# Group C's guests spread over more beats of the projection, and decode's page numbers read ahead of their wait

## What is computed

```python
h = rms_norm(x, norm_g)
proj = jnp.einsum('btd,dn->btn', h, w_in)
(aq, ak, av, az, bq, bkv, bg, bz, cqk, cv, cif, co, cz) = jnp.split(proj, splits, axis=-1)
...
oa = diff_attention(...)                                  # group A, paged cache in decode
o_cs, o_win = compressed + selected, banded window        # group B
...
for j in range(CONV_W):                                   # group C: causal convolution, 4 taps
    acc = acc + xp[:, j:j + T].astype(f32) * c_conv_w[j].astype(f32)
qk_c = jax.nn.silu(acc)
...
hc, (C1, n1, m1) = mlstm_chunkwise(qc, kc, vc, gif[:, :, 0], gif[:, :, 1], C0, n0, m0)
...
y = x + jnp.einsum('btm,md->btd', mix, w_out)
```

## Time and profile before

| | before |
|---|---|
| median of 3 runs (lowest to highest) | 2131.74 us (2131.07 to 2131.77) |
| profiled execution, its own time | 2134.85 us |
| its span | 2133.1 us |
| PE busy | 1754.7 us (82%) |
| PE weight loads busy | 1350.9 us (63%) |
| DVE busy | 819.9 us (38%) |
| ACT busy | 590.2 us (28%) |
| POOL busy | 81.1 us (4%) |
| HBM over the span | 170 GB/s |

### The profile page before, as it was taken

The page is one execution under the profiler, slowest core; times in us unless marked ns, Lnnn a source line. Parts: engine busy times, 40 slices in busy tenths (PEclk is TensorE's granted clock), DMA queues, the critical chain, the costliest instruction groups (busy, mean ns, idle before and its releaser), DMA issues. The chain is left out here.

```text
span 2133.1 us, 39056 instructions
## 1 busy us (share of the span) xinstructions
PE 1754.7 (82%) x14961; PEld 1350.9 (63%) x14961; DVE 819.9 (38%) x1592; ACT 590.2 (28%) x1352; POOL 81.1 (4%) x130
## 2 busy tenths in 40 slices
PE   7999999999886889879927975877787777647999
PEld 5888887888664556666716664555665655426776
DVE  4222212222264421234255752444455544646221
ACT  4211111112122102111134320444444444343110
POOL 3000000000000000000022010000000000021000
PEclk9999999999998877789967975999999999869999
DMA  6555655543322111132361002999899999455233
GB/s 198 175 185 182 189 159 184 179 135 105 125 83 66 59 44 60 55 87 82 100 254 54 29 21 82 361 341 337 311 331 329 355 321 331 166 195 192 80 122 110
DMA packets 213184, 361.28 MB, mean 169 GB/s; under 512 B 41229, under 2 KB 121566, under 8 KB 211142
## 3 DMA queue, kind: packets, MB, share of 16 engines
q1 hardware_dynamic: 212214, 356.16, 49.4%
q10 hardware_dynamic: 288, 2.10, 0.3%
q0 software_dynamic: 496, 0.53, 0.1%
HBM read 326.18 MB, written 36.79 MB: 170 GB/s over the span
## 5 line engine op out<-in xcount | busy, mean ns | idle before, releaser
L364 PE MATMUL pj_ps<-pj_whi,pj_xhi 128*128 128x512 f32 (+1 forms) x1024 | 420.9, 411 | 9.6 <-PEq L84 7.3
L365 PE MATMUL pj_ps<-pj_wlo,pj_xhi 128*128 128x512 f32 (+1 forms) x1024 | 404.7, 395 | 0.0
L366 PE MATMUL pj_ps<-pj_whi,pj_xlo 128*128 128x512 f32 (+1 forms) x1024 | 404.0, 395 | 0.0
L282 DVE TENSOR_TENSOR pj_wlo<-pj_w,pj_whi 128x1024 fp32r<-128x1024 f32 (+1 forms) x128 | 153.1, 1197 | 542.7 <-ACT pj_whi L242 540.3
L242 ACT ACTIVATE pj_whi<-pj_w 128x1024 fp32r<-128x1024 f32 (+1 forms) x128 | 132.6, 1036 | 578.7 <-DMA pj_w<-in_w_in 578.6
L364 PEld LDWEIGHTS pj_ps<-pj_whi,pj_xhi 128*128 128x128 f32 x1024 | 200.1, 195 | 70.3 <-issue 32.0
L366 PEld LDWEIGHTS pj_ps<-pj_whi,pj_xlo 128*128 128x128 f32 x1024 | 199.6, 195 | 41.2
L365 PEld LDWEIGHTS pj_ps<-pj_wlo,pj_xhi 128*128 128x128 f32 x1024 | 200.8, 196 | 34.5
L1347 PE MATMUL da_tp<-all_ident,da_pa 128*128 128x128 f32 x1024 | 156.1, 301 | 78.2 <-DMA da_pb<-in_cache_b_kv 76.7
L1467 ACT ACTIVATE da_kT<-da_tp 128x512 f32<-128x512 f32 x200 | 119.2, 596 | 263.0 <-PE da_tp L1347 263.0
L1347 PEld LDWEIGHTS da_tp<-all_ident,da_pa 128*128 128x128 f32 x1024 | 125.5, 154 | 99.5 <-DMA da_pb<-in_cache_b_kv 87.4
(11 more groups left out here) (513 smaller groups left out, 2231.8 us busy)
## 6 DMA issues: line engine op xcount, KB each, us to landing
da_pa<-in_cache_a_kv SPq DMA_DIRECT2D x256, 512.0 KB, 5.7
pj_w<-in_w_in SPq DMA_DIRECT2D x120, 512.0 KB, 4.6
px_pages<-in_cache_b_kv SPq DMA_DIRECT2D x256, 128.0 KB, 2.4
da_pb<-in_cache_b_kv SPq DMA_DIRECT2D x256, 128.0 KB, 6.1
ou_w<-in_w_out SPq DMA_DIRECT2D x32, 512.0 KB, 4.1
proj<-pj_out SPq DMA_DIRECT2D x52, 256.0 KB, 3.5
ap_rows_p<-proj SPq DMA_DIRECT2D x4, 1408.0 KB, 14.6
da_pw<-in_state_b_win SPq DMA_DIRECT2D x8, 512.0 KB, 7.8
```

The costliest lines, as they stand in the source:

```text
L282: dve.tensor_tensor(self.wlo[:, r, :, 0:n], self.w[:, r, :, 0:n], self.whi[:, r, :, 0:n], ALU.subtract).then_inc(self.wlo_ready, 1)
L364: pe.matmul(acc, hi, high, start=kc == 0, stop=False)
L365: pe.matmul(acc, hi, low, start=False, stop=False)
L366: last = pe.matmul(acc, lo, high, start=False, stop=kc == KC - 1)
```

## The change

It has five parts. (1) Decode: SP reads a group's four page numbers before it waits for `summed`, not behind. (2) `Convolve` has slots 80 to 99: its first four jobs come after 3 beats, the other ten after 20; the taps are 32 steps of one channel with a `yield` behind three of four, 24 beats in all; PE, ACT and DVE count their beats to match. (3) `PromptMemory` has slots 100 to 115: units follow each other every 5 beats (UNITBEATS) in place of 3, HEADBEATS goes from 9 to 11, PE and ACT start two beats later, PE gets a beat more behind the scores and behind the sums, and DVE makes denominator and output first, and the state (L2269, L2273 after) and mp_ncabd (L2207 after) one beat later. (4) `SampleMemory` has slots 116 to 127 and starts after 8 beats in place of 4. (5) The ranges of slots. No operation is added or taken away; `tapped` is raised 32 times in place of 8.

```diff
--- before.py
+++ after.py
@@ -1258,13 +1258,13 @@
                 for n, (b, what, p) in enumerate(steps):
                     if what == "page":
                         m = b * NG + p
+                        _, pages = nc.values_load_multi_w_load_instructions(
+                            table[0:1, 4 * m:4 * m + 4], engines=[mybir.EngineType.SP],
+                            min_val=0, max_val=d.cache_b.shape[0] - 1)
                         if m >= RING:
                             old = next(x for x in range(N) if steps[x][1] == "page"
                                        and steps[x][0] * NG + steps[x][2] == m - RING)
                             sp.wait_ge(summed, old + 1)
-                        _, pages = nc.values_load_multi_w_load_instructions(
-                            table[0:1, 4 * m:4 * m + 4], engines=[mybir.EngineType.SP],
-                            min_val=0, max_val=d.cache_b.shape[0] - 1)
                         for i in range(4):
                             sp.dma_start(pa[:, m % RING, i, :], d.cache_a[bass.ds(pages[i], 1), :, :]
                                          .rearrange("a p n -> p (a n)")).then_inc(loaded[m % RING], 16)
...
@@ -1817,16 +1816,20 @@
             yield
         sp.wait_ge(self.stored, 16 * (DB + 1))
 
-    START = 14
+    EARLY, START, TAPS = 3, 20, 24
+
+    def pause(self, n):
+
+        return self.EARLY if n == 0 else self.START - self.EARLY - 4 if n == 4 else 0
 
     def pool(self, pool):
         return iter(())
 
     def pe(self, pe):
         k = self.k
-        for _ in range(self.START):
-            yield
         for n, (what, t, h) in enumerate(self.JOBS):
+            for _ in range(self.pause(n)):
+                yield
             if what == "w":
                 pe.wait_ge(self.w_loaded, 48)
                 src, rows = self.w, 5
@@ -1856,7 +1859,7 @@
                                 k.ident[0:NS, 0:NS])
         last.then_inc(self.g_turned, 1)
         yield
-        for _ in range(8 + 4):
+        for _ in range(self.TAPS + 4 + 2):
             yield
         for t, (r0, rows) in enumerate(TILES):
             if t == 0:
@@ -1871,16 +1874,16 @@
 
     def act(self, act):
         k = self.k
-        for _ in range(self.START + self.N + 3):
+        for _ in range(self.START + self.N - 4 + 3):
             yield
         act.wait_ge(self.f_ready, 1)
         act.activation(self.t1[:], self.t0[:], ACT.Exp).then_inc(self.f_exped, 1)
         act.wait_ge(self.f_exped, 1)
         act.activation(self.t1[:], self.t1[:], ACT.Ln, bias=1.0).then_inc(self.f_logged, 1)
-        for _ in range(8):
+        for _ in range(self.TAPS):
             yield
         for x in range(4):
-            act.wait_ge(self.tapped, 8)
+            act.wait_ge(self.tapped, 32)
             if x:
                 act.wait_ge(self.silu_done, x)
             act.activation(self.sig[:], k.qkT[:, 2 * x:2 * x + 2, :], ACT.Sigmoid).then_inc(self.sig_done, 1)
@@ -1919,20 +1922,20 @@
         dve.scalar_tensor_tensor(self.t0[:], k.gate_f[:], -1.0, k.gate_f[:], ALU.mult, ALU.min).then_inc(self.f_ready, 1)
         yield
         dve.wait_ge(self.copied, self.N)
-        for x in range(8):
-            j, c0 = x // 2, 4 * (x % 2)
+        for x in range(32):
+            j, c = x // 8, x % 8
             if j:
-                dve.wait_ge(self.tapped, x - 1)
-            for c in range(c0, c0 + 4):
-                outs = ((k.qkT[:, c, 0:SEQ], self.xp[:, c, j:j + SEQ]),
-                        (k.qkT[:, c, SEQ:ROWS].rearrange("p (b t) -> p b t", b=DB), self.xs[:, c, :, j:j + DT]))
-                for out, src in outs:
-                    if j == 0:
-                        last = dve.tensor_scalar(out, src, self.wT[:, c, 0:1], self.wT[:, c, 4:5], ALU.mult, ALU.add)
-                    else:
-                        last = dve.scalar_tensor_tensor(out, src, self.wT[:, c, j:j + 1], out, ALU.mult, ALU.add)
+                dve.wait_ge(self.tapped, x - 7)
+            outs = ((k.qkT[:, c, 0:SEQ], self.xp[:, c, j:j + SEQ]),
+                    (k.qkT[:, c, SEQ:ROWS].rearrange("p (b t) -> p b t", b=DB), self.xs[:, c, :, j:j + DT]))
+            for out, src in outs:
+                if j == 0:
+                    last = dve.tensor_scalar(out, src, self.wT[:, c, 0:1], self.wT[:, c, 4:5], ALU.mult, ALU.add)
+                else:
+                    last = dve.scalar_tensor_tensor(out, src, self.wT[:, c, j:j + 1], out, ALU.mult, ALU.add)
             last.then_inc(self.tapped, 1)
-            yield
+            if x % 4:
+                yield
         dve.wait_ge(self.f_logged, 1)
         step(dve.tensor_scalar(k.gate_f[:], k.gate_f[:], 0.0, None, ALU.min))
         step(dve.tensor_tensor(k.gate_f[:], k.gate_f[:], self.t1[:], ALU.subtract))
@@ -2163,9 +2172,8 @@
                 h = 4 * hf + x
                 last = act.activation(self.w[:, x, :], self.bx[:, P * x:P * x + P], ACT.Exp, bias=self.col[:, c, 0, h:h + 1])
             last.then_inc(self.exped, 1)
-            yield
-            yield
-            yield
+            for _ in range(self.UNITBEATS):
+                yield
 
     def dve(self, dve):
         k, V = self.k, self.V
...
@@ -2237,20 +2247,12 @@
             dve.tensor_tensor(self.w[:], self.by[:].rearrange("p (x n) -> p x n", x=4), self.w[:],
                               ALU.mult).then_inc(self.weighed, 1)
             yield
+            yield
             dve.wait_ge(self.summed, u + 1)
-            for y in range(2):
-                half = slice(DC * y, DC * y + DC)
-                sy = self.S[half, 2 * hf:2 * hf + 2, :]
-                last = dve.tensor_tensor(sy, sy, self.csb[half, c, 4 * hf + y:4 * hf + 4:2].unsqueeze(2).broadcast_to(
-                    [DC, 2, V]), ALU.mult)
             nums = [b[:, 0:2 * V].rearrange("p (x n) -> p x n", x=2) for b in (self.bx, self.by)]
             for y in range(2):
-                dve.tensor_copy(self.den[:, 0, y:4:2].unsqueeze(2), nums[y][:, :, HEAD:V])
+                last = dve.tensor_copy(self.den[:, 0, y:4:2].unsqueeze(2), nums[y][:, :, HEAD:V])
             step(last)
-            st = self.S[:, 2 * hf:2 * hf + 2, :]
-            dve.tensor_tensor(st, st, self.bz[:, 0:2 * V].rearrange("p (x n) -> p x n", x=2),
-                              ALU.add).then_inc(self.state_ready, 1)
-            dve.wait_ge(self.state_ready, u + 1)
             step(dve.scalar_tensor_tensor(self.den[:, 1, :], self.den[:, 0, :], -1.0, self.den[:, 0, :], ALU.mult, ALU.max))
             step(dve.tensor_tensor(self.den[:, 1, :], self.den[:, 1, :], self.col[:, c, 1, 4 * hf:4 * hf + 4], ALU.max))
             step(dve.reciprocal(self.den[:, 2, :], self.den[:, 1, :]))
@@ -2260,6 +2262,16 @@
                 last = dve.tensor_tensor(self.h_out[:, y:4:2, :], nums[y][:, :, 0:HEAD],
                                          self.den[:, 2, y:4:2].unsqueeze(2).broadcast_to([P, 2, HEAD]), ALU.mult)
             last.then_inc(self.h_ready, 1)
+            yield
+            for y in range(2):
+                half = slice(DC * y, DC * y + DC)
+                sy = self.S[half, 2 * hf:2 * hf + 2, :]
+                last = dve.tensor_tensor(sy, sy, self.csb[half, c, 4 * hf + y:4 * hf + 4:2].unsqueeze(2).broadcast_to(
+                    [DC, 2, V]), ALU.mult)
+            step(last)
+            st = self.S[:, 2 * hf:2 * hf + 2, :]
+            dve.tensor_tensor(st, st, self.bz[:, 0:2 * V].rearrange("p (x n) -> p x n", x=2),
+                              ALU.add).then_inc(self.state_ready, 1)
             if u + 1 < len(self.UNITS):
                 block_rows(u + 1)
             if hf and c + 2 < PT:
...
@@ -2406,7 +2419,7 @@
 
     def pe(self, pe):
         k, V = self.k, self.V
-        for _ in range(4):
+        for _ in range(self.START):
             yield
         pe.wait_ge(self.made, 12)
         pe.wait_ge(self.st_loaded, 16 * (DB + 3))
...
@@ -2502,6 +2515,8 @@
         k, V = self.k, self.V
         step = Chain(dve, self.dve_step)
         row, nca, m = self.row, self.nca, self.m
+        for _ in range(self.START - 4):
+            yield
         dve.wait_ge(self.st_loaded, 16 * (DB + 3))
         dve.wait_ge(self.made, 12)
         for i in range(DB):
@@ -3014 +3029 @@
                     with Stage(nc, "cv") as g:
-                        hosted(nc, host, 80, 96, Convolve(nc, d, k, host, g))
+                        hosted(nc, host, 80, 100, Convolve(nc, d, k, host, g))
                     with Stage(nc, "mp") as g:
-                        hosted(nc, host, 96, 112, PromptMemory(nc, d, k, host, g))
+                        hosted(nc, host, 100, 116, PromptMemory(nc, d, k, host, g))
                 with Stage(nc, "md") as g:
-                    hosted(nc, host, 112, 128, SampleMemory(nc, d, k, host, g))
+                    hosted(nc, host, 116, 128, SampleMemory(nc, d, k, host, g))
         with Stage(nc, "at") as a:
             k.ones = a.sb("ones", [P, P])
             k.causal = a.sb("causal", [P, P])
```

18 lines of the change are left out of this document (12 added, 6 removed).

## The result

| | before | after |
|---|---|---|
| median (lowest to highest) | 2131.76 (2131.07 to 2133.02), 4 runs | 2042.97 (2037.88 to 2047.66), 4 runs |
| ratio, with its 95% interval | | 0.9582 (0.9556 to 0.9609) |
| span of the profiled execution | 2133.1 | 2043.8 |
| PE busy | 1754.7 | 1722.4 |

What follows compares the result with a forecast made beforehand. The prediction took PE to bound the shared stretch and transfers to bound decode. Terms -19 - 5 - 4 - 9 - 14 = -51 took the profiled 2134.85 to 2084, hence 2081 against the median; range 2060 to 2112.

Steps and rivals of the forecast that it cites:

- the key transposes: Convolve: PE's wait for the convolution's last product would be 7.0 us in place of 23.1.
- the handovers with a split: PromptMemory units ending in slots 106 and 112: an even slot's split delays the state, PE waits 5.3 us each.
- those without: PromptMemory's four unit handovers with nothing in between: PE waits 0.95 us each.
- PromptMemory's end: At slot 116 PE waits about 5.7 us, through SP's stores and the meeting of the engines.
- SampleMemory's first steps: SampleMemory: the wait for the samples' states falls from 7.0 to 2.2 us; next steps wait 2.5, 1.6, 1.9 and 1.0.
- the stretch of jobs: Convolve's first transposes: PE's wait of 8.6 us becomes 3.4, with 1.6 more at a beat behind an even slot's split.
- the rivals: Four alternatives: short waits harmless (12%), PromptMemory and clock give nothing (14%), decode bound by bytes (9%), lower clock holds through PromptMemory (5%).
- I take them as without effect: PromptMemory's clock: the four waits of 0.95 us bring no lower clock; clock term -9 over all guests.
- the first rival: PE's clock: short waits leave it alone, so the clock gives about 20 us more: gain 71, 2061; chance 12%.
- the full rate came back after 6.8 us each time: PromptMemory before: argument against rival 4, that with one wait in three tiles PE's lower clock lasted 6.8 us each.
- Where the share stays at 0.9 nothing is won: Decode: earlier issue pays only at 12 or 14 spots with DMA share under 0.5; term -14, of 0 to -17.
- two crossings of 5.3 us: PromptMemory: with output before state, an even slot's split stands between them in two units, costing PE 5.3 us each.

Runs made afterwards that it cites:

- the run with the numbers twice ahead: Kernel before with the decode part alone, but page numbers loaded twice, both times ahead of the wait for `summed`: 2147.04 us, ratio 1.0046.
- the run with the waits put in: Changed kernel with mp_ncabd made behind the output instead of behind the state, and three times over: 2031.3 us, ratio 0.9514 against the kernel before.

## Why the prediction was right and wrong

**What held.** The places where PE would wait, and for how long, came out nearly as worked out, but for one: the key transposes 5.9 (forecast 7.0), the handovers with a split between 5.4 and 4.3 (5.3 each), those without 0.87 (0.95), PromptMemory's end 5.65 (5.7), SampleMemory's first steps 1.5, 2.3 and 1.6 (2.2, 2.5 and 1.6). The one is the stretch of jobs, 7.0 and 1.6 (3.4 and 1.6). There I had taken the issue of the weights at 571.08 as fixed. It came at 577.58, 4.4 us later when measured from the start of the shared stretch: the four early jobs make PE's slots ahead of it longer, and SP waits for PE (its longest wait for L330 there is 13.3 us in place of 9.9). PE's idle time fell by 32.4, where the steps gave 28, and some of that is luck: Convolve gave 16.0 and not 19, PromptMemory with its end 10.3 and not 5 (two of seven handovers did not wait at all, and the entry cost less), SampleMemory 6.1 and not 4. None of the rivals came true as stated.

**What failed, first: "I take them as without effect", the clock.** The term was -9: four low stretches fewer in PromptMemory at 3.4 us each, one more in Convolve, at most one more in SampleMemory. Measured are -26.9 of busy time: -20.5 in PromptMemory (206.9 to 186.3), -1.4 in Convolve and -5.0 in SampleMemory, where I had +3 and +1. The price was nearly right, the count was not. There were 17 stretches at the lower level before (3, 11 and 3 by guest) and 10 after (2, 6 and 2), seven fewer and not two or three, which makes 3.8 us of busy time for each. The rule that I counted by, every wait from 1.1 us on and none below, was misread. Before already, in the shared stretch five waits between 1.4 and 2.0 us have no such stretch behind them (those that end at 538.24, 687.96, 883.40, 965.36 and 1029.49), not two. After, of twelve waits between 0.98 and 1.65 us only one has (the one before L2141 at 747.32), while of the three of 0.87 two have, and all seven above 2 us. So the first rival had the clock's size (-29 in all) for a reason that holds for most short waits and not for those of 0.87. The stretches are not of one length either, as "the full rate came back after 6.8 us each time" had it: in PromptMemory they last from 3.4 to 20.5 us before, and the longest (the window from 855.00 above) has two waits, of 2.96 us at its start and of 1.16 in its midst; after, none is longer than 10.2. What tells a wait with a low stretch from one without stays open. Both waits of 0.87 with one stand before a group of small matmuls, but so does the third. What the runs show is that with the five waits at the handovers gone the busy time falls by another 14.4.

**Second: "Where the share stays at 0.9 nothing is won", decode.** The term was -14, with 16.8 as its bound; measured are -32.6, and with the part alone -34.6 between the first and the last page DMA. The price of the load, 1.35, was right (1.57 to 0.21). The number of places was not. I had capped each place by the idle time of the DMA engines in two-us windows, and left out those whose share stays near 0.9. But 29 handovers waited, and 29 x 1.35 = 39 is near what came: of twenty stretches of 20 us from 1380 on, 16 had a DMA share below 1, down to 0.78, with 0.92 in the mean, and the mean rose to 0.98. So the stretch was not full at 0.92. That the other half of the gain came out of such small shortfalls fits this, and was not traced place by place. The first case of the Trainium skill's list in "Perfetto Trace Analysis", section "What "DMA-bound" means" (the DMA engines themselves bind) holds for the changed kernel, at 0.98, but not for the one before, at 0.92. Its second, the issuing sequencer, is what the run with the numbers twice ahead comes nearest to, with 7.7 of 8.1 us a group on SP, of which 2.9 are the loads and not DMA issues. Of "TensorE: Matmul & The Clock Gate", section "HAM oscillation — how this bites in real kernels", also in the Trainium skill, which ties the lower rate to long gaps, the waits of 0.87 and 1.07 with slow matmuls behind them are the exception here: they are not long gaps.

**Third, a part whose sign I had not priced.** I took the exchange of output and state as neutral apart from two crossings of 5.3 us. The run with the state first (20 us faster) shows that the crossings, and the low stretches behind them, cost 15.6 us of the window. The change won in spite of this hunk.

The sum with the measured terms: -32.4 idle, -26.9 clock, -32.6 decode, +2.6 for the rest = -89.3. Of the 38 us by which the forecast missed, 18 are the clock, 19 are decode, 4 are waits, and 3 the other way are the rest.

## What to carry to other kernels

When PE is the bound and waits often for a short time, count the busy time of the same matmuls in both versions beside the idle time: here nearly half of the gain in the shared stretch was busy time, and the cheapest remedy was to make the small operand that PE waits for (mp_ncabd) as soon as its buffer is free, ahead of longer work on the same engine. In a ring of transfers, price what stands between a wait and the next issue at every handover that waits, and look at the issuer's whole work a round as well: here a second load of 1.35 us cost 0.7 us a group, behind the wait and ahead of it alike.

## What was not expected of the hardware

A wait of 0.87 us before a group of small matmuls can be followed by matmuls at half rate, for 3.4 us in the case above (797.45). The price of such a wait varies: low stretches of 3.4 to 10.2 us were common, and behind waits of 1.15 and 1.83 us there were ones of 20 and 24 us in two profiled executions (the window above at 0.50, and 974.5 to 998.3 in the run with the waits put in), while in others, the changed kernel's at 991.37 among them, the same wait of 1.15 has none. Repeated runs of the changed kernel lay between 2037.88 and 2047.66, those of the kernel before within 2 us at first and between 2126 and 2143 in later sets. That such long stretches are what spreads them is likely and was not tested.
